# The first weight unit of a decoder layer: finer transfers, the squares of x on ScalarE, matmuls on zeros, products reordered

## The chip, the cores and the metric

The kernel runs on one core of a Trainium2 chip. The metric is the device time of one execution in microseconds, the median of several runs. The profile is of one execution.

## What is computed

One decoder layer on x of 512 tokens by 1024 channels, float32: a half-weighted SwiGLU feed-forward with 2816 hidden channels, a mixing part (gated linear attention and dilated attention side by side), a second feed-forward, and a final norm. What matters here is how it begins:

```python
def rms_norm(x, g):
    xf = x.astype(jnp.float32)
    y = xf * lax.rsqrt(jnp.mean(xf * xf, axis=-1, keepdims=True) + EPS)
    return (y * g.astype(jnp.float32)).astype(x.dtype)

def swiglu(x, w1, w3, w2):
    return (jax.nn.silu(x @ w1) * (x @ w3)) @ w2

x = x + 0.5 * swiglu(rms_norm(x, ffn1_norm[l]), ffn1_w1[l], ffn1_w3[l], ffn1_w2[l])
```

## The kernel before

x is held transposed, as 8 positions of 128 channels by 512 tokens. A float32 product is made of three: both sides are split into a high part, rounded to the matmul's type, and the rest, and hi by hi, hi by lo and lo by hi are added up in a PSUM bank (`product`, L968 to 972). So a tile of output, 128 channels by 512 tokens, takes 8 positions of three matmuls (`tile_of`, L974).

Weights come in units of 1 MB (in the first feed-forward: 128 rows of 2048 columns, the first 1024 for w1, the rest for w3). SyncE loads them alternately into `raw[0]` and `raw[1]` (`load`, L267), each as soon as VectorE has split the unit before it in that buffer (semaphore `w_split`). ScalarE rounds a unit to `w_hi` (`split`, L369 to 371; counted by `w_round`), VectorE subtracts to get `w_lo` (L590, 591; counted by `w_split`), and TensorE runs through the unit's two tiles. Units 0 and 1 use banks 0 to 3, unit 2 uses bank 0 again, so it needs VectorE to have emptied that (`tile_out`).

The norm's factor is applied behind the matmul: h is x times the gain only (`round_h` on ScalarE, L381, `low_h` on VectorE, L600), and VectorE multiplies each finished bank by `rstd` (L631, 633). `rstd` needs the sum of squares of x over channels: squares of positions 0 to 3 on ScalarE (L438), added by VectorE (L681); squares of positions 4 to 7 and their additions on GpSimd (L321 to 327); then two products with a matrix of ones behind unit 0 or 1 (L1012, 1014), mean (L617), root (L393), reciprocal (L621), and the clearing of `sumsq` (L607).

Then every tile pair goes gate (L631), silu on ScalarE (L402), prod (L633, 636), rounding and rest of the hidden value (L405, L639). In this step ScalarE (`split_next` in `up`, L403) and VectorE (L637) also split the unit two ahead. Each engine runs its instructions in the written order, so unit 2's split stands behind the mean, the reciprocal and the first gate.

At the start SyncE issues seven transfers: the first half of unit 0 (L277), x as four pairs of positions (L279), the second half of unit 0 (L281), unit 1 (L271), and then constants, `w_a2` and the positions (L283 to 285). ScalarE issues the gains (L428). ScalarE rounds the first half of unit 0 (L430), then the eight h_hi (L383), the second half (L436), four squares (L438), unit 1. VectorE does w_lo of the first half (L669), the eight h_lo (L603), w_lo of the second half (L674), three additions (L681), unit 1. GpSimd computes, behind the sums, the tables for the rotary embedding (L331 to 345).

## Time and profile before

| | |
|---|---|
| median of 3 runs | 1035.94 us (1035.8 to 1037.5) |
| span of the profiled execution | 1035.7 us |
| TensorE busy | 1011.0 us (98%), 4500 matmuls |
| VectorE busy | 497.5 us (48%) |
| ScalarE busy | 333.9 us (32%) |
| GpSimd busy | 67.4 us (7%) |
| DMA | 92.36 MB, mean 89 GB/s |
| mean granted clock of TensorE | 0.993 |

Busy shares are over the whole span. The busy time of TensorE counts from the first matmul of an overlapping run to the end of its last, so it is not the time at its peak. In the timeline, a row gives the start, the time it took, engine and line, what was written from what, and in brackets how long the engine had been idle and whose end released it.

### The profile page before, as it was taken

The numbers are of one execution on the slowest core, as the hardware profiler recorded it, in microseconds if no ns is written. First come the engines' busy times: TensorE is split into PE (matmuls) and PEld (weight loads), VectorE is DVE, ScalarE is ACT, GpSimd is POOL, SyncE is SP. The second block draws the span as 40 slices with busy tenths as digits, with TensorE's granted clock in tenths as the row PEclk, the third lists the DMA queues.
The fourth block names the chain that finished last, engine by engine and source line by source line (L and its number), as shares of the span: only waits on it lengthen the run. The fifth ranks groups of instructions, "written<-read, shape, count | busy, mean of one in ns | idle before, by whom it ended". The sixth has DMA issues, their size and how long they took to land.

```text
span 1035.7 us, 11866 instructions
## 1 busy us (share of the span) xinstructions
PE 1011.0 (98%) x4500; PEld 807.9 (78%) x4500; DVE 497.5 (48%) x641; ACT 333.9 (32%) x412; POOL 67.4 (7%) x47
## 2 busy tenths in 40 slices
PE   5999999999999999999999999999999999999995
PEld 4788888888888877888776577888888888888884
DVE  7654442244443455734267755854534234444343
ACT  5333321122322345412435533533322113222220
POOL 4850000000000000000122110000000000000000
PEclk9999999999999999999999999999999999999997
DMA  6323222323221323222120012232222232221222
GB/s 250 122 81 114 78 72 102 113 90 122 81 79 64 101 101 122 83 87 90 68 81 1 2 41 82 82 122 81 86 96 87 95 112 92 109 95 57 74 72 81
DMA packets 16272, 92.36 MB, mean 89 GB/s; under 512 B 1888, under 2 KB 1904, under 8 KB 8688
## 3 DMA queue, kind: packets, MB, share of 16 engines
q1 hardware_dynamic: 15520, 90.86, 24.8%
q10 hardware_dynamic: 720, 1.07, 0.3%
q8 instruction: 21, 0.34, 0.1%
q14 instruction: 11, 0.09, 0.0%
HBM read 89.82 MB, written 2.10 MB: 89 GB/s over the span
## 4 chain that ended last, share of the span: by engine, by line
PE 95%; DVE 3%; ACT 1%; DMA 0%; issue 0%; DVEq 0%; ACTq 0%
PE bank L970 29%; PE bank L972 28%; PE bank L971 28%; PE bank L1164 2%; PE bank L1152 2%; PE bank L1176 2%; DVE h_lo L603 1%; PE bank L1105 1%; DVE w_lo L591 1%; DMA raw<-in_up 0%; DVE x L962 0%; PE bank L1101 0%; PE bank L1182 0%; DVE rstd L621 0%; PE bank L1074 0%
## 5 line engine op out<-in xcount | busy, mean ns | idle before, releaser
L970 PE MATMUL bank<-h_hi,w_hi 128*128 128x512 f32 x904 | 356.9, 395 | 12.8 <-DVE h_lo L603 10.2
L971 PE MATMUL bank<-h_lo,w_hi 128*128 128x512 f32 x904 | 353.3, 391 | 0.0
L972 PE MATMUL bank<-h_hi,w_lo 128*128 128x512 f32 x904 | 353.3, 391 | 0.0
L371 ACT ACTIVATE w_hi<-raw 128x2048 fp32r<-128x2048 f32 (+2 forms) x92 | 158.0, 1717 | 336.3 <-PE bank L972 336.3
L591 DVE TENSOR_TENSOR w_lo<-raw,w_hi 128x2048 fp32r<-128x2048 f32 (+2 forms) x92 | 189.0, 2054 | 90.6 <-ACT w_hi L371 90.3
L970 PEld LDWEIGHTS bank<-h_hi,w_hi 128*128 128x128 f32 x904 | 170.6, 189 | 55.0 <-DVE w_lo L669 9.0
L972 PEld LDWEIGHTS bank<-h_hi,w_lo 128*128 128x128 f32 x904 | 170.5, 189 | 36.2
L971 PEld LDWEIGHTS bank<-h_lo,w_hi 128*128 128x128 f32 x904 | 170.7, 189 | 35.2 <-issue 0.7
L972 PE MATMUL bank<-g_hi,w_lo 128*128 128x512 f32 x352 | 140.4, 399 | 0.0
L971 PE MATMUL bank<-g_lo,w_hi 128*128 128x512 f32 x352 | 138.7, 394 | 0.0
L970 PE MATMUL bank<-g_hi,w_hi 128*128 128x512 f32 x352 | 138.0, 392 | 0.0
L633 DVE TENSOR_TENSOR prod<-bank,rstd 128x512 f32<-128x512 f32 x44 | 30.4, 691 | 188.1 <-PE bank L972 188.1
L646 DVE SCALAR_TENSOR_TENSOR x<-bank,x 128x512 f32 (+1 forms) x32 | 22.1, 691 | 124.2 <-PE bank L972 124.2
L971 PEld LDWEIGHTS bank<-g_lo,w_hi 128*128 128x128 f32 x352 | 66.1, 188 | 16.9
L970 PEld LDWEIGHTS bank<-g_hi,w_hi 128*128 128x128 f32 x352 | 66.1, 188 | 15.9
L972 PEld LDWEIGHTS bank<-g_hi,w_lo 128*128 128x128 f32 x352 | 66.1, 188 | 15.3
L402 ACT ACTIVATE gate<-gate 128x512 f32<-128x512 f32 x44 | 27.8, 632 | 155.4 <-DVE gate L631 155.4
L352 POOL TENSOR_TENSOR projT<-projT,rope_c 128x512 f32<-128x512 f32 x8 | 13.7, 1732 | 478.9 <-DVE square L726 478.1
L631 DVE TENSOR_TENSOR gate<-bank,rstd 128x512 f32<-128x512 f32 x44 | 30.3, 688 | 27.6 <-PE bank L972 26.7
L639 DVE TENSOR_TENSOR g_lo<-prod,g_hi 128x512 f32 (+1 forms) x44 | 33.1, 752 | 0.0
L636 DVE TENSOR_TENSOR prod<-prod,gate 128x512 f32<-128x512 f32 x44 | 30.5, 693 | 2.5 <-ACT gate L402 0.6
L389 ACT ACTIVATE square<-x 128x512 f32 (+1 forms) x24 | 15.0, 625 | 48.8 <-DVE x L646 41.7
(176 smaller groups left out, 661.4 us busy)
## 6 DMA issues: line engine op xcount, KB each, us to landing
raw<-in_up SPq DMA_DIRECT2D x43, 1024.0 KB, 4.7
raw<-in_w_proj SPq DMA_DIRECT2D x8, 1024.0 KB, 4.8
raw<-in_down1a SPq DMA_DIRECT2D x8, 768.0 KB, 4.3
raw<-in_down2a SPq DMA_DIRECT2D x8, 768.0 KB, 4.3
raw<-in_down1b SPq DMA_DIRECT2D x8, 640.0 KB, 3.8
raw<-in_down2b SPq DMA_DIRECT2D x8, 640.0 KB, 3.9
raw<-in_w_v SPq DMA_DIRECT2D x4, 1024.0 KB, 4.8
raw<-in_w_o SPq DMA_DIRECT2D x4, 1024.0 KB, 4.8
```

The lines of the kernel that those rows point to most:

```text
L371: nc.scalar.activation(w_hi[u % 2][:, 0:size], raw[u % 2][:, 0:size], ACT.Copy).then_inc(w_round, 1)
L402: nc.scalar.activation(gate[:], gate[:], ACT.Silu).then_inc(silu_done, 1)
L591: nc.vector.tensor_tensor(w_lo[u % 2][:, 0:size], raw[u % 2][:, 0:size], w_hi[u % 2][:, 0:size].bitcast(F32), ALU.subtract).then_inc(w_spl ...
L631: nc.vector.tensor_tensor(gate[:], ps[2 * j][:], rstd[:], ALU.mult).then_inc(tile_out, 1)
L633: nc.vector.tensor_tensor(prod[:], ps[2 * j + 1][:], rstd[:], ALU.mult).then_inc(tile_out, 1)
L636: nc.vector.tensor_tensor(prod[:], prod[:], gate[:], ALU.mult).then_inc(g_mul, 1)
L639: nc.vector.tensor_tensor(g_lo[:, f, :], prod[:], g_hi[:, f, :].bitcast(F32), ALU.subtract).then_inc(g_ready, 1)
L646: nc.vector.scalar_tensor_tensor(x[:, m, :], ps[4 + j][:], 0.5, x[:, m, :], ALU.mult, ALU.add).then_inc(tile_out, 1)
L970: nc.tensor.matmul(out, a_hi, b_hi, start=first, stop=False)
L971: nc.tensor.matmul(out, a_hi, b_lo, start=False, stop=False)
L972: return nc.tensor.matmul(out, a_lo, b_hi, start=False, stop=last)
L1152: nc.tensor.matmul(ps[4 + i % 2][:, 0:(i + 1) * P], projT[r:r + HD, T_AQ + 2 * (h // 2), i * P:(i + 1) * P], projT[r:r + HD, T_AK + 2 * (h ...
```

## The change

- The first half of unit 0 comes in two transfers, of 256 and 768 columns, and x in eight transfers of one position each. The order is w part 0, x0, w part 1, x1, x2 to x7, then as before. Each part and each position has its own semaphore.
- ScalarE rounds part 0, then h_hi 0, part 1, h_hi 1, and the rest of h_hi; VectorE follows in the same order.
- GpSimd squares nothing. ScalarE squares positions 0 and 1 ahead of unit 1 and positions 2 to 7 behind it, into eight buffers; VectorE adds all up, seven additions, behind w_lo of unit 1. One product with ones, behind the first tile of unit 1, sums them.
- Unit 2's split stands on both engines ahead of the norm's mean and the first gate, no more in the first `up` step. The first two `up` steps are written out ahead of the loop.
- VectorE clears `rope_c`, and TensorE multiplies it three times into bank 7, which nothing reads, ahead of the first product.
- In unit 0's first tile, TensorE does hi by hi of position k+1 ahead of the two products with lo of position k. In the next two tiles all products with `w_hi` stand ahead of those with `w_lo`, so that only these wait for `w_split`.

```diff
-        first_squares = [sumsq, square, rstd, ffn_mem[1][2]]
+        first_squares = [sumsq, square, rstd, ffn_mem[1][2], ffn_mem[1][3], rope_s, part, turn]
+        FIRST_COLS = ((0, 2 * P), (2 * P, D))
...
-                    sp.dma_start(raw[0][:, 0:D], source(0)[:, 0:D]).then_inc(w_first, 16)
-                    for j in range(4):
-                        sp.dma_start(x[:, 2 * j:2 * j + 2, :],
-                                     xT_in[2 * j:2 * j + 2].rearrange("c p s -> p c s")).then_inc(x_in[j], 16)
+                    for j, (lo, hi) in enumerate(FIRST_COLS):
+                        sp.dma_start(raw[0][:, lo:hi], source(0)[:, lo:hi]).then_inc(w_first[j], 16)
+                        sp.dma_start(x[:, j, :], xT_in[j]).then_inc(x_in[j], 16)
+                    for m in range(2, KC):
+                        sp.dma_start(x[:, m, :], xT_in[m]).then_inc(x_in[m], 16)
...
-            for m in range(KC // 2, KC):
-                pool.wait_ge(x_in[m // 2], 16)
-                if m == KC // 2:
-                    step(nc.gpsimd.tensor_tensor(rope_s[:], x[:, m, :], x[:, m, :], ALU.mult))
-                else:
-                    step(nc.gpsimd.tensor_tensor(part[:], x[:, m, :], x[:, m, :], ALU.mult))
-                    step(nc.gpsimd.tensor_tensor(rope_s[:], rope_s[:], part[:], ALU.add))
...
             act.wait_ge(w_in[0], 16)
             nc.scalar.activation(w_hi[0][:, D:UP_W], raw[0][:, D:UP_W], ACT.Copy).then_inc(w_round, 1)
-            for m, out in enumerate(first_squares):
-                nc.scalar.activation(out[:], x[:, m, :], ACT.Square).then_inc(first_sq, 1)
+            for m in range(2):
+                square_first(m)
             split(1, 0, unit_size(1))
+            for m in range(2, KC):
+                square_first(m)
+            split_next(0, 0, 2)
             ffn(0, 0, 0, ffn_mem[1][0], ffn_mem[1][2], ffn_mem[1][3], G_MIX)
...
+            nc.vector.memset(rope_c[:], 0.0).then_inc(warm_zero, 1)
...
-            for m in range(1, KC // 2):
+            split(1, 0, unit_size(1))
+            for m in range(1, KC):
                 dve.wait_ge(first_sq, m + 1)
                 if m > 1:
                     dve.wait_ge(first_sum, m - 1)
                 nc.vector.tensor_tensor(sumsq[:], sumsq[:], first_squares[m][:], ALU.add).then_inc(first_sum, 1)
-            split(1, 0, unit_size(1))
+            split_next(0, 0)
             ffn(0, 0, 0, *ffn_mem[1], G_MIX)
...
+                    def first_unit():
+
+                        for pos in range(KC + 1):
+                            if pos < KC:
+                                pe.wait_ge(first_round, min(pos // 2 + 1, 2))
+                                pe.wait_ge(h_round, pos + 1)
+                                nc.tensor.matmul(ps[0][:], w_hi[0][:, pos * P:pos * P + P], h_hi[:, pos, :],
+                                                 start=pos == 0, stop=False)
+                            if pos:
+                                k = pos - 1
+                                pe.wait_ge(first_split, min(k // 2 + 1, 2))
+                                pe.wait_ge(h_ready, k + 1)
+                                nc.tensor.matmul(ps[0][:], w_hi[0][:, k * P:k * P + P], h_lo[:, k, :],
+                                                 start=False, stop=False)
+                                last = nc.tensor.matmul(ps[0][:], w_lo[0][:, k * P:k * P + P], h_hi[:, k, :],
+                                                        start=False, stop=k == KC - 1)
+                        last.then_inc(tile_done, 1)
+                        pe.wait_ge(tile_out, BANK_CREDIT)
+                        late_low(0, 1, 1, lambda: pe.wait_ge(w_round, 1), lambda: pe.wait_ge(w_split, 1))
+
+                    def late_low(slot, w, bank, rounded, split):
+
+                        rounded()
+                        for k in range(KC):
+                            col = (w * KC + k) * P
+                            nc.tensor.matmul(ps[bank][:], w_hi[slot][:, col:col + P], h_hi[:, k, :],
+                                             start=k == 0, stop=False)
+                            nc.tensor.matmul(ps[bank][:], w_hi[slot][:, col:col + P], h_lo[:, k, :],
+                                             start=False, stop=False)
+                        split()
+                        for k in range(KC):
+                            col = (w * KC + k) * P
+                            last = nc.tensor.matmul(ps[bank][:], w_lo[slot][:, col:col + P], h_hi[:, k, :],
+                                                    start=False, stop=k == KC - 1)
+                        last.then_inc(tile_done, 1)
+
+                    def second_unit():
+
+                        late_low(1, 0, 2, lambda: pe.wait_ge(w_round, 2), lambda: pe.wait_ge(w_split, 2))
+                        pe.wait_ge(const_landed, 32)
+                        pe.wait_ge(first_sum, KC - 1)
+                        channel_sums(0, 6, sumsq[:])
+                        tile_of(1, 1, 3)
...
+            pe.wait_ge(warm_zero, 1)
+            for _ in range(WARM):
+                nc.tensor.matmul(ps[7][:], rope_c[:, 0:P], rope_c[:], start=True, stop=True)
             ffn(0, 0, 0, *ffn_mem[1])
```

## Rows read from the trace of the kernel before

**Rows 1.** The page: TensorE's busy time, and its costliest group of instructions.
```profile
PE 1011.0 (98%) x4500; PEld 807.9 (78%) x4500; DVE 497.5 (48%) x641; ACT 333.9 (32%) x412; POOL 67.4 (7%) x47
...
L970 PE MATMUL bank<-h_hi,w_hi 128*128 128x512 f32 x904 | 356.9, 395 | 12.8 <-DVE h_lo L603 10.2
```
**Rows 2.** The timeline, TensorE (PE matmul, PEld weight load), 9 to 41 us.
```profile
9.02 0.77 PE L970 MATMUL bank<-h_hi,w_hi 128*128 128x512 f32 x1 [9.02 <-DVE h_lo L603]
...
14.84 0.19 PEld L970 LDWEIGHTS bank<-h_hi,w_hi 128*128 128x128 f32 x1 [0.43 <-DVE h_lo L603]
...
19.97 0.19 PEld L970 LDWEIGHTS bank<-h_hi,w_hi 128*128 128x128 f32 x1 [1.45 <-DVE w_lo L674]
...
27.17 1.02 PE L1012 MATMUL bank<-sumsq,const 128*128 128x512 f32 x2
...
40.59 0.19 PEld L970 LDWEIGHTS bank<-h_hi,w_hi 128*128 128x128 f32 x1 [1.04 <-issue]
```
**Rows 3.** The waits of 0 to 60 us (in total, times, longest).
```profile
PE bank L970 <- DVE h_lo L603: 10.2, 3, 9.0
```
**Rows 4.** VectorE: line 603's durations (ns min/median/max), then the timeline, 21 to 45 us.
```profile
L603 DVE SCALAR_TENSOR_TENSOR h_lo<-x,gains,h_hi x8: 746/1524/1776, 8.1 to 16.2; 128x512 fp32r<-128x512 f32 x8
...
21.71 0.69 DVE L681 TENSOR_TENSOR sumsq<-sumsq,rstd 128x512 f32<-128x512 f32 x1
22.51 0.69 DVE L681 TENSOR_TENSOR sumsq<-sumsq,gate 128x512 f32<-128x512 f32 x1
23.12 2.29 DVE L591 TENSOR_TENSOR w_lo<-raw,w_hi 128x2048 fp32r<-128x2048 f32 x1
29.08 0.69 DVE L617 TENSOR_SCALAR rstd<-bank 128x512 f32<-128x512 f32 x1 [3.68 <-PE bank L1014]
...
34.40 0.63 DVE L631 TENSOR_TENSOR gate<-bank,rstd 128x512 f32<-128x512 f32 x1
...
37.53 2.92 DVE L591 TENSOR_TENSOR w_lo<-raw,w_hi 128x2048 fp32r<-128x2048 f32 x1 [0.95 <-ACT w_hi L371]
...
44.80 2.29 DVE L591 TENSOR_TENSOR w_lo<-raw,w_hi 128x2048 fp32r<-128x2048 f32 x1 [1.02 <-ACT w_hi L371]
```
**Rows 5.** The timeline, GpSimd, its first work on x.
```profile
10.04 1.05 POOL L324 TENSOR_TENSOR rope_s<-x 128x512 f32<-128x512 f32 x1 [9.61 <-DMA x<-in_xT]
```
**Rows 6.** Windows of 1 us: busy by engine, granted clock (PEclk), DMA share, GB/s.
```profile
21.00:22.00 1.00, 1.00 (x4) 0.79 (x3) 0.89 (x2) 0.00 (x0) 0.05 (x1) 0.50 0.80 172
...
23.00:24.00 1.00, 1.00 (x4) 0.76 (x4) 1.00 (x2) 0.00 (x0) 0.00 (x0) 0.56 0.95 401
```
**Rows 7.** Transfers: issues of L279 (x), L271 (units from 1 on), landing of gains last.
```profile
L279 SPq DMA_DIRECT2D x<-in_xT x4: 423/517/585, 1.2 to 2.8; - x4
...
DMA to landing us min/median/max: 6.1/7.4/8.5
...
L271 SPq DMA_DIRECT2D raw<-in_up x6: 333/338/576, 4.1 to 56.3; - x6
...
DMA to landing us min/median/max: 4.7/4.7/11.0
...
DMA to landing us min/median/max: 5.3/5.3/5.3
```
**Rows 8.** Windows of 1 us, columns as in rows 6, two early microseconds.
```profile
2.00:3.00 1.00, 0.00 (x0) 0.00 (x0) 0.00 (x0) 0.47 (x1) 0.00 (x0) 1.00 0.90 247
...
10.00:11.00 1.00, 1.00 (x4) 0.80 (x3) 1.00 (x2) 1.00 (x2) 0.96 (x1) 1.00 1.07 422
```
**Rows 9.** The timeline, ScalarE, 7 to 18 us.
```profile
7.34 5.32 ACT L383 ACTIVATE h_hi<-x,gains 128x512 fp32r<-128x512 f32 x8 [0.39 <-DMA x<-in_xT]
12.60 1.06 ACT L436 ACTIVATE w_hi<-raw 128x1024 fp32r<-128x1024 f32 x1
13.57 0.61 ACT L438 ACTIVATE sumsq<-x 128x512 f32<-128x512 f32 x1
...
15.65 1.89 ACT L371 ACTIVATE w_hi<-raw 128x2048 fp32r<-128x2048 f32 x1
```

More of the change, by code:

```diff
@@ L153, in layer_program @@
         ps = [ctx.enter_context(nc.psum_tensor(f"bank{b}", [P, S], F32)) for b in range(8)]
-        x_in = [sem(f"x_in{j}") for j in range(4)]
+        x_in = [sem(f"x_in{j}") for j in range(KC)]
         gains_in_sem = sem("gains_landed")
         const_landed = sem("const_landed")
-        w_first = sem("w_first")
+        w_first = [sem(f"w_first{j}") for j in range(2)]
+        warm_zero = sem("warm_zero")
         pos_landed = sem("pos_landed")
@@ L659, in ffn @@
                         clear_sums()
-                    with dve.Fori(0, n // 2 - 1) as i:
+                    peeled = u0 == 0
+                    if peeled:
+                        up(0, 0, True)
+                        up(0, 1)
+                    with dve.Fori(int(peeled), n // 2 - 1) as i:
                         for j in range(2):
@@ L1007, in up @@
                                 channel_sums(NORM[layer], 6, sumsq[:])
-                        if first and layer == 0:
-                            pe.wait_ge(const_landed, 32)
-                            pe.wait_ge(first_sum, KC // 2 - 1)
-                            nc.tensor.matmul(ps[6][:], ones, sumsq[:], start=True, stop=False)
-                            pe.wait_ge(pool_step, KC - 1)
-                            nc.tensor.matmul(ps[6][:], ones, rope_s[:], start=False, stop=True).then_inc(sums_done, 1)
+                    def first_unit():
[16 more added lines that the diff above has]
+                        late_low(0, 1, 1, lambda: pe.wait_ge(w_round, 1), lambda: pe.wait_ge(w_split, 1))
```

53 lines of the change are left out of this document (33 added, 20 removed).

## The prediction

> **What bounds the kernel now.** I read the page first, then the waits, then the first 60 us of the timeline engine by engine. The page says that TensorE is busy for 1011.0 of 1035.7 us [rows 1]: outside a few places it is the bound, and whatever brings it sooner into its unbroken run shifts all that follows by the same amount. One matmul costs 1011.0 / 4500 = 0.225 us of that, though the line's mean is 395 ns [rows 1], because they overlap; a unit of 48 costs 10.8 us. The diff touches only what lies before unit 2 of the weights, so the question is one number: when does TensorE start on unit 2? In the timeline it starts on unit 0 at 9.02, and starts on unit 2 at 40.59, after a gap of 1.04 [rows 2]. Units 0 and 1 hold 96 matmuls, 96 x 0.225 = 21.6 us, and the sums of squares some 2 us (two products of about 1 us, the first at 27.17) [rows 2]: 24 us of work in 31.6 us of time. The rest is waiting, and the low clock.
>
> The waits name the cause: of the 10.2 us that TensorE waited for h_lo, 9.0 lie before the first matmul [rows 3], and then each position waits for VectorE. VectorE needs 1524 ns in the median for one h_lo, 746 at best and 1776 at worst [rows 4]. The long ones lie where GpSimd is at work on its squares, from 10.04 on [rows 5]. The Trainium skill ("SBUF — State Buffer", the section on the two separate sides) says that a VectorE instruction with two SBUF inputs and a GpSimd instruction that reads SBUF hold a shared pair of ports for their whole length, so that one blocks the other. By that, the trace agrees: the median h_lo is a GpSimd operation longer than the shortest, or nearly so.
>
> The clock plays a part too. TensorE's gaps between the last positions grew from 0.43 us at 14.84 to 1.45 at 19.97 (four in all) [rows 2], and behind them the granted clock reads 0.50, that is 1.2 GHz, at 21 to 22 us, and 0.56 in the microsecond from 23 to 24 [rows 6]. At that level a unit costs twice as much.
>
> At 40.59 what released TensorE was w_lo of unit 2, a 2.92 us subtraction that began at 37.53 [rows 4]. It was queued on ScalarE and VectorE behind the norm and the first gate. So today two chains set the start of unit 2: this split, and the chain sums, mean, root, reciprocal, first gate, which frees bank 0 (from 29.08 to 34.40 + 0.63 = 35.03) [rows 4].
>
> **The change part by part.** I follow the bytes, then ScalarE, VectorE and TensorE.
>
> Transfers. Up to the end of unit 1 the same 4.19 MB move, in 12 transfers instead of 7. In the trace the x pairs were issued from 1.2 to 2.8 us and landed 6.1 to 8.5 us after issue, so x was whole at about 11.3; unit 1 was issued at 4.1 and took 11.0 us, so it landed at 15.1 [rows 7]. An issue takes 0.42 to 0.59 us [rows 7]; ten more of these ahead of unit 1 put its issue near 6 us, far ahead of its bytes, so the rate of the queue remains the limit and I leave 15.1 where it is. The first quarter of w (0.13 MB) and x0 (0.26 MB) land earlier than the first 0.52 MB did; but the gains, which took 5.3 us [rows 7] from an issue at 0.73, land at 6.0, and h_hi of position 0 needs them. The rate was 247 GB/s at 2 to 3 us and 422 at 10 to 11 [rows 8]. The Trainium skill ("DMA: Bandwidth & Descriptors", Bandwidth) speaks against finer transfers: batch to at least 1 MiB for three quarters of the peak. The trace's 512 KB transfers, queued back to back, moved at the 422 GB/s, so by the row the sum does not change; by the rule it is the second rival below.
>
> ScalarE. h_hi of position 0 runs from 6.05 to 6.7 (eight took 5.32, 0.66 each) [rows 9], the rest of w_hi's first half needs 0.8, then seven h_hi of 0.66: done at 12.2, just behind the last x. The second half of w_hi stays at 12.60 [rows 9], for its bytes come no sooner. Two squares at 0.52 apart (four between 13.57 and 15.65) [rows 9] end at 14.7. Unit 1 now starts when it lands, 15.1, and takes 1.89 [rows 9]: 17.0. Six squares more: 20.2. These six are the four of GpSimd and two of ScalarE's own that stood ahead before; moved behind unit 1 they delay nobody, since VectorE is busy until 19.3. Unit 2's load waits for w_lo of unit 0 (now near 14.9 instead of 19.9) and takes 4.7 us at best [rows 7], with some 0.8 MB of constants and positions still ahead of it: 2 us at 422 GB/s, so it lands near 21. Its rounding ends at about 22.9.
>
> VectorE. Without GpSimd, h_lo goes at its minimum of 746 ns; eight of them and the two pieces of w_lo end at 13.6 instead of 17.9, and w_lo's second half at 14.9. Then unit 1: 17.1 plus 2.29 [rows 4] gives 19.3. The seven additions, 0.80 apart (21.71 to 22.51) [rows 4], where three stood before, start at 19.3, the last at 24.1: four more on the path, 3.2 us, is the price of taking the squares from GpSimd. Unit 2's split starts 0.61 behind the last one's start (as 23.12 behind 22.51) [rows 4] and takes 2.29: 27.0. Then comes the mean, and from the mean's start to the end of the first gate it takes the 5.95 us of today (29.08 to 35.03) [rows 4], GpSimd's rope table running beside it in both cases: **32.95**.
>
> TensorE. The three products on zeros run from about 1.4 to 6.5 at the worst: a whole fp32 product takes about 1.0 us [rows 2], twice that at 1.2 GHz. They end before h_hi of position 0 at 6.7, so they cost nothing; and they may bring the clock up. From 8.2 on (h_hi of position 1) a position costs 3 x 0.225 = 0.68 of TensorE and 0.75 of VectorE, so TensorE keeps pace. Tile 0 ends at 14.2, tile 1 at 19.6, tile 2 at 25.0, the sum at 26.0 and tile 3 at 31.4. The hi products ahead of the split matter little for the end: they cover that w_lo of unit 0's second half comes at 14.9 and unit 1's at 19.3. If the clock were low until 12 us, TensorE would end unit 1 at about 32.6, still inside its cover of 1.6 us; without that cover each lost us counts.
>
> The sum: unit 2 needs its split (27.0), TensorE (31.4) and bank 0 (32.95). The last decides: TensorE starts at 33.0 instead of 40.59, **7.6 us sooner**. Next to be late would be unit 3's split. Today w_lo of unit 3 starts 10.4 us behind the first gate's start (34.40 to 44.80) [rows 4]; with the split of unit 2 gone from between (2.9 and its wait of 0.95 less, g_hi's wait of 0.7 more) that is some 7.8, and its end 10 to 11 us behind the gate's start at 32.3: 42.4 to 43.4. TensorE wants it at 33.0 + 10.8 = 43.8. It fits, with GpSimd's collisions as the danger; I give it 0 to 0.8 us. The profiled span of 1035.7 is 0.24 below the median of the runs, 1035.94. Against the span the result is 1028.1, against the median **1028.4**.
>
> **The rivals.**
> The clock falls in the new gap. TensorE idles from 31.4 to 33.0. For: at 21 us the clock was 0.50 after four gaps of 0.4 to 1.5 us [rows 2, 6]. Against: the 1.04 us gap before 40.59 [rows 2] brought no fall, and here there is one gap, not four. The low level began in the microsecond behind 19.97, and with 0.56 from 23 to 24 [rows 6] it ended near 23.9: some 3.5 us, which at half speed cost 1.7. Result 1030.1 to 1030.6.
>
> The transfers are slower. If unit 2's load took the 11.0 us of unit 1 [rows 7] rather than 6, it would land at 26, be rounded at 28 and split at 30.3; with the 5.95 us behind it, 36.3: a gain of 4.3. The same comes out if fine transfers keep the 247 GB/s of the start [rows 8] up to 3.15 MB: 14.7 instead of 11, so all is 3.7 us later. Against: the rate rose while transfers of the same 2 KB rows were in flight. Result 1032.
>
> Better than forecast: unit 1 lands sooner, or VectorE's additions are closer together than 0.80. TensorE's own end of unit 1, 31.4, is the floor: 1026.8.
>
> Nothing comes of it: the start of unit 2 stays where it was, because VectorE, with four more additions and the split ahead of the mean, hands bank 0 over late. This needs 7 us on a chain that I put together from 14 durations of this trace: unlikely.
>
> Slower: the clock stays at 1.2 GHz through both units. The first matmul, at 9.02, has 0.77 us [rows 2], twice the mean of its line [rows 1]: TensorE starts slow. If the positions, paced by VectorE, never pack closely enough to end that, 95 matmuls from 8.2 at 0.45 and a doubled sum give 8.2 + 42.8 + 2 = 53.0, 12.4 later than today: 1048.3. It becomes slower than today once TensorE has lost more than 9.2 us against 31.4, that is with 41 matmuls more at the low level than the forecast has. Against: tiles 1 to 3 have all their inputs and run without gaps, and after the fall near 20 us such a run brought the clock back before 24 [rows 6].
>
> **How the numbers follow.** Forecast 0.58 (1027.4 to 1029.4), clock dip 0.17, slower transfers 0.10, better 0.07, nothing 0.04, slower 0.04. The range takes in the better case and the dip and ends inside the slower transfers: 1026.4 to 1031.6. A measurement of this kernel can tell about 0.2% (2 us) from no change. Faster by more than that: 0.58 + 0.17 + 0.10 + 0.07 = 0.92; within it 0.04; slower 0.04.
>
> **What would show it.** In the profile after: h_lo at about 0.75 us each and no GpSimd before 26 us; w_lo of unit 1 at 17.1; seven additions from 19.3 to 24.8; w_lo of unit 2 at 24.7, ahead of the mean at 27.0; the first gate's end at 33; TensorE's first matmul of unit 2 right behind it, and a wait of about 1.5 us there that names VectorE's gate. From there every row stands 7.6 us earlier. It is wrong if unit 1 lands later than 15.5, if the clock reads 0.50 anywhere from 14 to 40 us, or if w_lo of unit 3 ends after 44.

## The result, and the profile after

The kernel before took 1036.72 us in the comparison (median of 4 runs, 1035.8 to 1037.63), the changed one 1030.06 us (4 runs, 1029.84 to 1030.88). The ratio is 0.994, with a 95% interval of 0.9926 to 0.9955. The forecast was 1028.4 with a range of 1026.4 to 1031.6: the direction and the range held, the size was 1.7 us too hopeful against this time. Against the 1035.94 us that stood at the outset the gain is 5.9 us, where 7.6 were forecast.

The profiled execution has a span of 1028.7 us. Its page, to be read beside [rows 1], gives busy time by engine, the line of the granted clock in 40 slices, and the costliest group:

```profile
PE 1012.5 (98%) x4504; PEld 807.9 (79%) x4504; DVE 494.0 (48%) x647; ACT 331.5 (32%) x413; POOL 57.4 (6%) x40
...
PEclk9999999999999999999999999999999999999997
...
L992 PE MATMUL bank<-h_hi,w_hi 128*128 128x512 f32 x880 | 345.4, 392 | 2.4 <-DVE gate L644 1.4
```

TensorE is busy for 1.5 us more, the products on zeros included. Its costliest line waits 2.4 us in all where it waited 12.8. The two are not quite alike, for the first three tiles' products now have lines of their own (880 of the 904 are left); but on those lines the matmuls wait only 0.4 us, for an h_hi, and nowhere in the first 60 us does TensorE wait for h_lo any more. The clock's digit is 9 (90% or more) in every slice but the last, to which I come back; the line reads the same in the kernel before, for a dip of 3 us does not show in slices of 26.

The timeline of TensorE in the changed kernel, to 33 us (the row gives the start, the time it took, the line, and in brackets the idle time before it and its releaser); the rows that it answers to are [rows 2]:

```profile
1.48 5.49 PE L1090 MATMUL bank<-rope_c 128*128 128x512 f32 x6 [1.48 <-DVE rope_c L686]
5.98 1.34 PE L1032 MATMUL bank<-h_hi,w_hi 128*128 128x512 f32 x1
...
30.80 0.39 PE L994 MATMUL bank<-h_hi,w_lo 128*128 128x512 f32 x1
...
32.58 0.19 PEld L992 LDWEIGHTS bank<-h_hi,w_hi 128*128 128x128 f32 x1 [1.81 <-DVE gate L644]
```

Unit 2 starts at 32.58 instead of 40.59 [rows 2], right behind the first gate and behind the longest gap of the beginning, 1.81 us. The waits name the same releaser (engine and line, waited for whom: in total, times, longest):

```profile
PEld bank L992 <- DVE gate L644: 1.8, 1, 1.8
...
PE bank L992 <- DVE gate L644: 1.4, 1, 1.4
```

VectorE in the changed kernel, the rows that answer to [rows 4]:

```profile
7.86 4.73 DVE L616 SCALAR_TENSOR_TENSOR h_lo<-x,gains,h_hi 128x512 fp32r<-128x512 f32 x7
...
16.78 2.29 DVE L604 TENSOR_TENSOR w_lo<-raw,w_hi 128x2048 fp32r<-128x2048 f32 x1 [2.12 <-ACT w_hi L369]
18.99 0.69 DVE L703 TENSOR_TENSOR sumsq<-sumsq,square 128x512 f32<-128x512 f32 x1
...
23.77 0.69 DVE L703 TENSOR_TENSOR sumsq<-sumsq,turn 128x512 f32<-128x512 f32 x1
24.38 2.29 DVE L604 TENSOR_TENSOR w_lo<-raw,w_hi 128x2048 fp32r<-128x2048 f32 x1
26.58 0.68 DVE L630 TENSOR_SCALAR rstd<-bank 128x512 f32<-128x512 f32 x1
...
31.89 0.63 DVE L644 TENSOR_TENSOR gate<-bank,rstd 128x512 f32<-128x512 f32 x1
...
39.40 2.29 DVE L604 TENSOR_TENSOR w_lo<-raw,w_hi 128x2048 fp32r<-128x2048 f32 x1 [1.11 <-ACT w_hi L369]
...
43.79 0.69 DVE L646 TENSOR_TENSOR prod<-bank,rstd 128x512 f32<-128x512 f32 x1
```

Seven h_lo take 4.73 us with GpSimd idle; from the last addition to the end of the gate (31.89 + 0.63) every row stands 0.3 to 0.4 us ahead of the forecast and in its order. Against the kernel before the lead is 8.03 us at 43.79 (the same instruction stood at 51.82) and lasts until the final norm. There the two kernels part once more. Windows of 1 us, the changed kernel (busy share and count of PE, PEld, DVE, ACT, POOL, then the granted clock, DMA share, GB/s):

```profile
1013.00:1014.00 1.00, 0.61 (x6) 0.65 (x6) 0.00 (x0) 0.24 (x1) 0.00 (x0) 1.00 0.00 0
1014.00:1015.00 1.00, 1.00 (x7) 1.00 (x6) 0.00 (x0) 0.00 (x0) 0.00 (x0) 0.52 0.00 0
1015.00:1016.00 1.00, 1.00 (x7) 1.00 (x6) 0.00 (x0) 0.00 (x0) 0.00 (x0) 0.50 0.00 0
```

In the kernel before the clock fell 0.6 us behind the same sums, not inside them:

```profile
1022.00:1023.00 1.00, 1.00 (x11) 1.00 (x11) 0.00 (x0) 0.00 (x0) 0.00 (x0) 1.00 0.00 0
1023.00:1024.00 1.00, 0.36 (x4) 0.28 (x3) 0.33 (x2) 0.20 (x1) 0.00 (x0) 0.99 0.00 0
1024.00:1025.00 1.00, 0.00 (x0) 0.00 (x0) 0.86 (x6) 0.00 (x0) 0.00 (x0) 0.50 0.00 0
```

The sums of the final norm come 7 a microsecond instead of 11, and the lead shrinks from 8.03 to 7.01 us (the last products of the norm start at 1018.55, before at 1025.56). The other three executions of the changed kernel have spans of 1027.7, 1027.9 and 1027.9, some 0.9 shorter than the profiled one, and a mean granted clock of 0.994 against its 0.993; that these did not lose the microsecond at the end is inferred from the two.

### The profile page after: what moved, and what is told of

Same layout as the page of the kernel before. It is cut to its first block, busy times and chain, and to the rows that moved or that the text cites. A ratio compares the mean times of both kernels' runs of the same rounds, so it can differ in the third digit from the quotient of the medians.

```text
span 1028.7 us, 11872 instructions
## 1 busy us (share of the span) xinstructions
PE 1012.5 (98%) x4504; PEld 807.9 (79%) x4504; DVE 494.0 (48%) x647; ACT 331.5 (32%) x413; POOL 57.4 (6%) x40
## 4 chain that ended last, share of the span: by engine, by line
PE 95%; DVE 3%; DMA 1%; SPq 0%; ACT 0%; issue 0%; DVEq 0%; ACTq 0%
PE bank L992 29%; PE bank L994 28%; PE bank L993 28%; PE bank L1224 2%; PE bank L1212 2%; PE bank L1236 2%; DMA raw<-in_up 1%; PE bank L1165 1%; DVE w_lo L604 1%; DVE sumsq L703 0%; DVE x L984 0%; PE bank L1161 0%; PE bank L1242 0%; DVE rstd L634 0%; PE bank L1134 0%
## 5 line engine op out<-in xcount | busy, mean ns | idle before, releaser
L992 PE MATMUL bank<-h_hi,w_hi 128*128 128x512 f32 x880 | 345.4, 392 | 2.4 <-DVE gate L644 1.4
L993 PE MATMUL bank<-h_lo,w_hi 128*128 128x512 f32 x880 | 342.5, 389 | 0.0
L994 PE MATMUL bank<-h_hi,w_lo 128*128 128x512 f32 x880 | 342.5, 389 | 0.0
L992 PEld LDWEIGHTS bank<-h_hi,w_hi 128*128 128x128 f32 x880 | 165.2, 188 | 41.8 <-issue 3.1
L994 PEld LDWEIGHTS bank<-h_hi,w_lo 128*128 128x128 f32 x880 | 165.2, 188 | 34.4
L993 PEld LDWEIGHTS bank<-h_lo,w_hi 128*128 128x128 f32 x880 | 165.2, 188 | 34.4 <-issue 0.7
L993 PEld LDWEIGHTS bank<-g_lo,w_hi 128*128 128x128 f32 x352 | 66.1, 188 | 17.1
L387 ACT ACTIVATE square<-x 128x512 f32 (+1 forms) x24 | 15.0, 625 | 48.8 <-DVE x L660 41.7
```

The source lines that it names most:

```text
L992: nc.tensor.matmul(out, a_hi, b_hi, start=first, stop=False)
L993: nc.tensor.matmul(out, a_hi, b_lo, start=False, stop=False)
L994: return nc.tensor.matmul(out, a_lo, b_hi, start=False, stop=last)
```

## The experiments

Eleven variants were run, and the kernel before once more for a second trace of it. Every ratio is against the kernel before, run among the same runs. None leaves out a part of the layer's computation; the products at the end, like the zeros, write a bank that nobody reads, and GpSimd's early write is of a tile that is overwritten before use.

| | us, median | start of unit 2, us |
|---|---|---|
| before | 1035.8 to 1037.3 | 40.59 (39.04 in a second trace) |
| changed | 1030.06 | 32.58 |
| no products on zeros | 1031.42 | 32.75 |
| unit 2's split as before | 1037.3 | 37.10 |
| GpSimd squares again | 1035.06 | 38.12 |
| before, with the early split alone | 1035.86 | 39.67 |
| transfers as before | 1031.9 | 34.42 |
| products in the old order | 1030.47 | 32.87 |
| sums earlier | 1029.69 | 32.09 |
| products at the end | 1029.37 | as changed |
| sums earlier, constants later | 1028.47 | no gap left |
| all three | 1027.58 | no gap left |
| one early GpSimd write | 1030.33 | as changed |

### Without the products on zeros

```diff
-WARM = 3
+WARM = 0
```

> The changed kernel without the three products on zeros. In the changed kernel TensorE idles 1.81 us before unit 2 (from 30.77 to 32.58), waiting for the first gate; the zeros ran from 1.48 to 6.9 and the clock was full from the second real product on. Theory (the zeros buy a full clock early, and the idle time covers most of it): without them TensorE runs its first 4 us or more at 1.2 GHz, ends unit 1 some 2 us later, the sum of squares too, so the mean starts up to 1 us later than 26.58 and unit 2 begins at 33.0 to 33.6: 0.4 to 1.0 us slower than the changed kernel. Rival (zeros do nothing): unit 2 still begins at 32.6. Second rival (the clock never settles while positions are paced by VectorE): unit 2 begins after 36.

Measured: 1031.42 us (1030.62 to 1031.67), ratio 0.9955 (0.9938 to 0.9972). The timeline of TensorE:

```profile
8.05 0.77 PE L1032 MATMUL bank<-h_hi,w_hi 128*128 128x512 f32 x1 [1.81 <-ACT h_hi L381]
8.61 0.63 PE L1038 MATMUL bank<-h_lo,w_hi 128*128 128x512 f32 x1
9.04 0.63 PE L1040 MATMUL bank<-h_hi,w_lo 128*128 128x512 f32 x1
...
11.16 0.39 PE L1038 MATMUL bank<-h_lo,w_hi 128*128 128x512 f32 x1
11.39 0.39 PE L1040 MATMUL bank<-h_hi,w_lo 128*128 128x512 f32 x1
```

Until 11 us the products come 0.43 us apart, behind that 0.23. Half speed for 3 us costs TensorE 1.5 us, and in this execution nearly all of it lies inside idle time: unit 2 starts at 32.75, 0.17 later. But the cover is not the 1.6 us ahead of unit 2 alone. The mean needs the sum of squares, and this ended at 25.71 in the changed kernel, 0.9 us before the mean; here it ends at 26.71 and the mean starts at 26.75, so that any further loss of TensorE would delay mean, gate and unit 2 by the same amount. The profiled execution is the fastest of the four; the others are 0.5 to 1.0 longer in span. The likely reason, not shown, is that in these the half speed lasted longer: in the two traces of the kernel before it lasted until 13.4 us in one and 12.2 in the other. A different loss at the end of the kernel is the rival, and nothing here rules it out. The median is 1.4 us above that of the changed kernel, from four runs of each whose ranges overlap a little (1030.62 to 1031.67, 1029.84 to 1030.88), though the traced beginning says 0.2.

### Unit 2's split behind the first gate again

```diff
-                        up(0, 0, True)
+                        up(0, 0)
...
-            split_next(0, 0)
             ffn(0, 0, 0, *ffn_mem[1], G_MIX)
```

(The same edit on ScalarE.)

> The changed kernel with unit 2's split back at its old place, behind the norm and inside the first up step. Theory (this order is the largest single part): the mean starts when the sum of squares is out, 25.8 instead of 26.58, the first gate ends near 31.7, but the split follows it: ScalarE from 31.9 to 33.8, VectorE's subtraction from 33.8 to 36.1 or 36.7. Unit 2 begins at 36.2 to 37.2: 3.6 to 4.6 us slower than the changed kernel. Rival (the gate is what matters, the split is hidden beside it): unit 2 begins near 32, no slower.

Measured: 1037.3 us (10 runs, 1036.97 to 1038.18), ratio 1.0013 (1.0004 to 1.0023): slower than the kernel before. The wait, the split itself, and 1 us windows from 35 us:

```profile
PE bank L990 <- DVE w_lo L603: 6.0, 1, 6.0
```
```profile
34.14 2.83 DVE L603 TENSOR_TENSOR w_lo<-raw,w_hi 128x2048 fp32r<-128x2048 f32 x1 [1.01 <-ACT w_hi L369]
```
```profile
35.00:36.00 1.00, 0.00 (x0) 0.00 (x0) 1.00 (x1) 0.00 (x0) 1.00 (x1) 0.77 0.00 0
36.00:37.00 1.00, 0.00 (x0) 0.00 (x0) 1.00 (x2) 0.00 (x0) 1.00 (x1) 0.50 0.00 0
...
41.00:42.00 1.00, 1.00 (x4) 0.71 (x4) 0.80 (x1) 0.69 (x2) 0.92 (x2) 0.50 0.16 66
```

The split ends near 37.0 and unit 2 starts at 37.10, inside the expected range and 4.5 us later than with the whole change. The median is 7.2 us longer, though. During the wait (6.0 us without a product, 6.4 between weight loads) the clock falls, it reads 0.50 from 36 to 42 us, and TensorE's first 5.3 us of unit 2 run at half speed, which costs 2.65. 4.5 + 2.65 = 7.2. (The two traced spans are only 6.1 apart, for the traced changed kernel lost its 1.0 us at the end, and this one did not.) So the early split is the largest of the parts that were taken out one by one, and it is worth more than the wait that it removes.

### GpSimd squares positions 4 to 7 again

```diff
+            for m in range(KC // 2, KC):
+                pool.wait_ge(x_in[m], 16)
+                ...
-            for m in range(1, KC):
+            for m in range(1, KC // 2):
                 dve.wait_ge(first_sq, m + 1)
```

> The changed kernel with the squares of positions 4 to 7 back on GpSimd and two products with ones, three additions on VectorE instead of seven. Theory (GpSimd's work slows VectorE's h_lo): GpSimd works from about 8.7 to 18, h_lo goes from 0.69 to about 1.5 us each, the last ends near 16 instead of 12.6, the first tile near 16.7 instead of 13.2; TensorE passes the end of the sums some 4.5 us later (3.5 from the tile, 0.9 for the second product), so the mean starts near 30 and unit 2 begins at 35 to 36: 2.5 to 3.5 us slower. Rival (the four additions saved on VectorE, 3.2 us, pay for the slower h_lo): unit 2 begins within 0.5 us of 32.6.

(ScalarE's four squares and four of the additions go with it, and the second product with ones comes back.)

Measured: 1035.06 us (10 runs, 1033.53 to 1036.4), ratio 0.9984 (0.9975 to 0.9994). VectorE in this kernel, beside the 4.73 and 2.29 us of the changed one:

```profile
7.71 9.31 DVE L623 SCALAR_TENSOR_TENSOR h_lo<-x,gains,h_hi 128x512 fp32r<-128x512 f32 x7
...
18.93 3.37 DVE L611 TENSOR_TENSOR w_lo<-raw,w_hi 128x2048 fp32r<-128x2048 f32 x1
```

From one h_lo to the next it is 1.33 us against 0.68. That is the contention on which the prediction rested; the other things that this edit moves stand behind the h_lo, so it is GpSimd's work that lengthens them. The size was a miss: unit 2 starts 5.5 us later (38.12), not 2.5 to 3.5. The subtractions are lengthened too (3.37 for 2.29), and TensorE waits for each h_lo in turn, five times from 10 to 17 us. Behind these gaps the granted clock falls. The waits of 0 to 25 us, then the windows:

```profile
PE bank L1045 <- DVE h_lo L623: 3.2, 5, 1.0
```
```profile
17.00:18.00 1.00, 0.83 (x3) 0.71 (x4) 1.00 (x2) 0.99 (x2) 0.92 (x1) 0.73 0.05 18
18.00:19.00 1.00, 1.00 (x4) 0.81 (x3) 1.00 (x2) 0.00 (x0) 1.00 (x1) 0.50 0.00 0
...
20.00:21.00 1.00, 1.00 (x4) 0.77 (x3) 1.00 (x1) 0.00 (x0) 0.14 (x1) 0.57 0.76 131
```

The low time in the four windows from 17 to 21 adds up to 3.4 us, and half speed over that time costs 1.7.

### The kernel before with the early split alone

```diff
+                    peeled = u0 == 0
+                    if peeled:
+                        up(0, 0, True)
+                        up(0, 1)
...
+            split_next(0, 0)
             ffn(0, 0, 0, *ffn_mem[1], G_MIX)
```

> The kernel before with one part of the change alone: unit 2's split ahead of the mean and the first gate on both engines. Theory (the parts don't add up: alone, this one meets TensorE's own late end of unit 1 at 39.6): unit 2 begins at 39.6 to 39.8 instead of 40.59, 0.8 to 1.0 us faster than before, though the same order is worth 4 us in the changed kernel. Rival (the parts add up): 3.6 us or more faster than before. Second rival (the split ahead delays mean and gate by 2.3 us, and this decides): the gate ends at 37.3, before 39.6, so nothing is lost by it; if unit 2 begins later than 40.6 this is wrong.

Measured: 1035.86 us (10 runs, 1034.88 to 1036.6), ratio 0.9994 (0.9984 to 1.0003). The kernel before has two sorts of executions, with spans near 1034.1 and near 1035.7 (below). Here four of the ten spans are near 1033.1, three are 1034.8 and three lie between; the two ends are 0.9 to 1.0 us below those of the kernel before, as expected. In VectorE's rows the split now holds the mean up, since its load comes late, and the first gate follows:

```profile
29.39 2.62 DVE L597 TENSOR_TENSOR w_lo<-raw,w_hi 128x2048 fp32r<-128x2048 f32 x1 [3.88 <-ACT w_hi L371]
31.94 0.68 DVE L623 TENSOR_SCALAR rstd<-bank 128x512 f32<-128x512 f32 x1
...
37.24 0.63 DVE L637 TENSOR_TENSOR gate<-bank,rstd 128x512 f32<-128x512 f32 x1
```

TensorE's weight load for unit 2:

```profile
39.67 0.19 PEld L982 LDWEIGHTS bank<-h_hi,w_hi 128*128 128x128 f32 x1
```

The mean came at 29.08 before [rows 4]. But the split is done at 32.0 and the gate at 37.9, and neither decides: TensorE goes from unit 1 into unit 2 at 39.67 with no idle time in the row. What bounds this kernel is TensorE's own late way through units 0 and 1, which is why the early split alone brings 1 us. Taken out of the whole change it costs 7. The parts don't add up: the split pays in full only once TensorE itself is through unit 1 early.

### Transfers as before

```diff
-                    for j, (lo, hi) in enumerate(FIRST_COLS):
-                        ...
+                    sp.dma_start(raw[0][:, 0:D], source(0)[:, 0:D]).then_inc(w_first[0], 16)
+                    for j in range(4):
+                        sp.dma_start(x[:, 2 * j:2 * j + 2, :],
+                                     xT_in[2 * j:2 * j + 2].rearrange("c p s -> p c s")).then_inc(x_in[j], 16)
```

> The changed kernel with the transfers of before: the first half of unit 0 in one, x in four pairs. Theory (finer transfers start the chain sooner, but the chain that decides hangs on unit 1's landing): h_hi of position 0 starts near 7.3 instead of 4.54, the last h_lo ends near 14.2 instead of 12.6, unit 1 lands at 15.1 as before; TensorE passes the sum some 1.4 us later, so the mean starts 0.2 to 0.7 us later than 26.58 and unit 2 begins at 32.8 to 33.3: 0.2 to 0.7 us slower. Rival (fine transfers cost rate): unit 1 lands sooner with coarse ones and unit 2 begins before 32.6.

Measured: 1031.9 us (5 runs, 1031.32 to 1032.32), ratio 0.996 (0.9946 to 0.9974); unit 2 starts at 34.42, 1.84 later, where 0.2 to 0.7 were expected. The timeline of TensorE, then the windows:

```profile
1.48 5.25 PE L1089 MATMUL bank<-rope_c 128*128 128x512 f32 x6 [1.48 <-DVE rope_c L685]
8.25 0.47 PE L1031 MATMUL bank<-h_hi,w_hi 128*128 128x512 f32 x1 [1.53 <-ACT h_hi L380]
9.60 0.61 PE L1031 MATMUL bank<-h_hi,w_hi 128*128 128x512 f32 x1 [0.87 <-ACT h_hi L380]
```
```profile
9.00:10.00 1.00, 0.40 (x1) 0.39 (x2) 1.00 (x2) 1.00 (x3) 0.00 (x0) 0.88 1.07 412
10.00:11.00 1.00, 1.00 (x4) 0.79 (x3) 1.00 (x2) 1.00 (x3) 0.00 (x0) 0.50 1.08 428
```

The mean, on VectorE:

```profile
28.43 0.69 DVE L629 TENSOR_SCALAR rstd<-bank 128x512 f32<-128x512 f32 x1 [1.32 <-PE bank L1008]
```

The first product comes 2.3 us later than the 5.98 of the changed kernel, since the first bytes of x do: h_hi of position 0 starts at 7.39, there at 4.54. TensorE idles between the zeros and it, and once more behind it, and the clock, at 0.88 in the first window, reads 0.50 from 10 to 13 us. The bulk of the bytes is hardly late: unit 1's rounding starts at 15.27 here and at 14.83 in the changed kernel. Those 0.44 us carry through to the end of unit 2's split (27.11), and they are what the expected 0.2 to 0.7 was made of. The mean waits 1.32 us longer, for TensorE's sum of squares, and that wait is the rest of the 1.8. TensorE is late for two reasons, the last h_lo (14.48 instead of 12.59) and the clock (3.4 us low, of which some 1.5 us of delay are left, since h_lo would have held TensorE up a little even at full speed). Without the clock's part the sum, out at 28.39, would have been out at about 26.9, an estimate from these rows, ahead of the split. So most of what the finer transfers are worth here, some 1.3 of 1.8 us, comes from the clock, because TensorE is kept at work early. They lost nothing of the rate: 416 and 442 GB/s at 9 to 11 us with single positions, 412 and 428 with pairs.

### Products in the old order

First tile position by position, then `tile_of` for the others, as in the kernel before.

```diff
-                        late_low(1, 0, 2, lambda: pe.wait_ge(w_round, 2), lambda: pe.wait_ge(w_split, 2))
+                        pe.wait_ge(w_split, 2)
+                        tile_of(1, 0, 2)
```

> The changed kernel with the products in the old order: no hi product ahead, and tiles 1 and 2 wait for w_lo before they start. Theory: tile 1 waits for w_lo of unit 0's second half until 14.7 instead of starting at 13.3, so everything on TensorE is 1.2 to 1.5 us later up to the sum; the sum is out near 27.0 instead of 25.7, the mean 0.4 us later, unit 2 begins near 33.0: 0.4 us slower. Rival (the order is worth its full 1.4 us): unit 2 begins at 34. Second rival (nothing): 32.6.

Measured: 1030.47 us (4 runs, 1030.31 to 1031.04), ratio 0.9947 (0.993 to 0.9964). Unit 2 starts at 32.87, 0.3 later: tile 1 waits 1.46 us for its split and starts at 14.81, and this shows through only where the sums follow it. The new order is worth 0.3 to 0.4 us, which these runs (four of each) hardly tell from nothing.

### Sums earlier

From here on the experiments go beyond the change: what is late now is the chain sums, mean, gate. Three squares and two of the seven additions stand ahead of unit 1's split, the clearing of `sumsq` behind the gate, and the product with ones in the middle of tile 2.

```diff
+            for m in range(1, KC):
+                if m == 3:
+                    split(1, 0, unit_size(1))
...
+                            if k == KC // 2 and between:
+                                between()
```

> The changed kernel with its deciding chain shortened: squares 0 to 2 ahead of unit 1 on ScalarE, two of the seven additions in VectorE's idle time ahead of unit 1's split, the sum of squares taken in the middle of tile 2's products with w_lo, and the clearing of the sum behind the first gate instead of ahead of it. Theory (the chain additions, split of unit 2, mean, root, reciprocal, gate decides): the five additions end near 22.9 instead of 24.5, the mean starts near 25.1, the gate ends 2.0 us sooner, and TensorE, whose own end of unit 1 is 30.8, begins unit 2 at 30.8 to 31.2 instead of 32.58: 1.4 to 1.8 us faster than the changed kernel. Rival (the next to be late is unit 3's split, which ended at 41.7 where TensorE wanted it at 43.5): half of the gain is lost again at 41.7. Second rival: no gain, since TensorE was the bound.

Measured: 1029.69 us (4 runs, 1029.32 to 1030.07), ratio 0.9937 (0.992 to 0.9954). Unit 2 starts at 32.09, not at 30.8 to 31.2. The rows of ScalarE and VectorE name the new bound:

```profile
22.42 1.92 ACT L369 ACTIVATE w_hi<-raw 128x2048 fp32r<-128x2048 f32 x1 [2.83 <-DMA raw<-in_up]
```
```profile
24.37 2.29 DVE L604 TENSOR_TENSOR w_lo<-raw,w_hi 128x2048 fp32r<-128x2048 f32 x1 [1.26 <-ACT w_hi L369]
```

ScalarE had been idle for 2.83 us when unit 2's bytes landed at 22.4. In the changed kernel they landed at 20.7; why 1.7 us sooner there I did not settle. In both they stand in the queue behind 1.2 MB of constants and positions (the prediction had counted 0.8), and the next experiment takes those out of their way.

### Constants and positions behind unit 2

This stands on top of the sums earlier.

```diff
-                    sp.dma_start(const[:], const_in).then_inc(const_landed, 16)
+                    sp.dma_start(const[:, 0:C_STRIP], const_in[:, 0:C_STRIP]).then_inc(const_landed, 16)
...
+                    load(0, 1, source(2))
+                    sp.dma_start(const[:, C_STRIP:N_CONST], const_in[:, C_STRIP:N_CONST]).then_inc(const_rest, 16)
```

> The kernel with the sums taken earlier, and in addition all constants but the identity and the ones, and the positions, are loaded behind unit 2 of the weights instead of ahead of it. There, unit 2 landed at 22.4 us (VectorE idled 1.26 us for it) and TensorE began unit 2 at 32.09 instead of the 31.0 expected. Theory (unit 2's load is what came late, behind 1.05 MB nobody needs yet): it lands 2 us or more sooner, at 19.7 to 20.5, its split starts at 22.9 to 23.0, the mean when the sum is out, near 25.0, the gate ends near 30.5, and TensorE begins unit 2 at 30.9 to 31.2, with no wait or one of 0.2 us: 1.5 us faster than the changed kernel (0.9 faster than with the sums alone). Rival (unit 3's split, which ended at 41.3 there, now comes late, since its load moves behind the constants): TensorE waits at 41.8 to 42.5 and gives half of it back.

Measured: 1028.47 us (4 runs, 1028.42 to 1028.52), ratio 0.9923 (0.9908 to 0.9938), 1.6 below the changed kernel. Unit 2's rounding starts at 19.61 instead of 22.42, the mean at 25.09, the first gate at 29.86, and TensorE goes from tile 3 into unit 2 with no gap. TensorE's own work is the bound from 8 us on, the floor that the rival "better" of the prediction named; its time of 1026.8 is too low by the step that failed, as below. Unit 3's split, whose load now stands behind the constants, was in time: TensorE has no idle time there.

### Products that keep the clock up at the end

Seven products ahead of the last sums and nine behind them, into a bank that nobody reads:

```diff
+            idle_products(7)
             pe.wait_ge(sq_added, 9 * 2 + KC)
...
+            idle_products(9)
             spread(1, 6, ffn_mem[2][4])
```

> The changed kernel with products nobody reads in TensorE's two idle times at the very end, 7 ahead of the final sums and 9 ahead of the spread of the norm. In the changed kernel the granted clock fell at 1014.0, in the kernel before at 1024.0, and in the profiled pair 1.0 of 8.0 us of the lead was lost right there, since the eight sums ran at 0.43 instead of 0.22 apart. Theory (the clock falls in the tail and costs there): the sums stay at 0.22 and the spread takes 1.1 instead of 2.1 us; the whole is 1.0 to 2.0 us faster than the changed kernel. Rival (the extra products delay the sums): if the clock falls all the same, nine products at 0.43 take 3.9 us where 2.3 are idle, and the kernel is 1.6 us slower.

Measured: 1029.37 us (4 runs, 1029.02 to 1030.43), ratio 0.9939 (0.9922 to 0.9955), 0.7 below the changed kernel, where 1.0 to 2.0 were expected. The expectation was made from the profiled execution, which had lost a microsecond more at the end than the others. The last product of the norm, here and then in the changed kernel:

```profile
1017.64 1.16 PE L1277 MATMUL bank<-norm_diag,const 128*128 128x128 f32 x8
```
```profile
1018.55 2.08 PE L1277 MATMUL bank<-norm_diag,const 128*128 128x128 f32 x8 [2.21 <-DVE norm_diag L869]
```

Eight matmuls in 1.16 us against 2.08: the end of the kernel was running at the low clock (0.50 from 1015 us on), and with the unread products it reads 1.00 until 1023.

### All three

Sums earlier, constants later and the products at the end together.

> Sums earlier, constants later, and the products in the tail's idle time, together. Theory: the start gives 1.5 us against the changed kernel and the tail 0.7 (as measured alone), and the two don't touch: 2.2 us faster than the changed kernel, near 1027.9 us, 8 us faster than before. Rival: the time in the tail depends on where the clock falls, so the sum may be 1.2 to 3.0.

Measured: 1027.58 us (5 runs, 1027.41 to 1028.7), ratio 0.9914 (0.99 to 0.9927): 2.5 below the changed kernel, where 2.2 were expected. It beats both kernels. The products at the end are no guarantee: in the profiled run, the slowest of the five, the clock fell in spite of them (0.74, 0.50, 0.50 and 0.55 in the four windows from 1014 us).

### The kernel before, a second trace

> The kernel before, unchanged, profiled once more. Of 25 runs of it 18 took 1035.7 to 1036.1 us with spans near 1034.1, and 7 took 1037.3 to 1037.6 with spans near 1035.7. The profile on which the prediction rests has a span of 1035.7. Theory (that profile is of the longer sort, and the difference is the low clock from 20.5 to 23.9 us): a profile with a span of 1034.1 shows no clock of 0.50 between 14 and 30 us, and TensorE ends the sums of squares and unit 1 some 1.6 us sooner, with unit 2 starting near 38.9. Rival (the difference lies elsewhere, in the tail or the middle): unit 2 starts at 40.6 in the short sort too.

Measured: 1036.3 us (10 runs, 1035.75 to 1037.63), ratio 1.0001. Six of the ten have spans of 1034.0 to 1034.7, four of 1035.6 to 1035.8; among its runs beside the other experiments, 7 of 25, 1 of 8, 6 of 15 and 4 of 7 were of the longer sort. The profiled one here is of the shorter. Its windows, a weight load and the mean, to be held against [rows 6], [rows 2] and [rows 4]:

```profile
21.00:22.00 1.00, 1.00 (x7) 0.79 (x6) 0.89 (x2) 0.00 (x0) 0.13 (x1) 1.00 0.70 164
...
23.00:24.00 1.00, 1.00 (x6) 0.84 (x5) 1.00 (x2) 0.00 (x0) 0.00 (x0) 1.00 0.95 401
```
```profile
14.91 0.19 PEld L970 LDWEIGHTS bank<-h_hi,w_hi 128*128 128x128 f32 x1 [1.13 <-DVE h_lo L603]
```
```profile
27.53 0.69 DVE L617 TENSOR_SCALAR rstd<-bank 128x512 f32<-128x512 f32 x1 [2.05 <-PE bank L1014]
```

No 0.50 here: seven matmuls from 21 to 22 us where the first trace had four. The mean comes 1.55 us earlier, and unit 2 starts at 39.04 instead of 40.59, so the dip accounts for 1.55 of the 1.6 us between the two traced spans. That it also parts the executions that were not traced is inferred from their spans. The gaps are alike except the first, 1.13 us here and 0.43 at 14.84 there [rows 2]: the half speed of the start ended sooner in this execution (12.2 against 13.4 us), so TensorE waited longer for h_lo. The execution with the longer idle time is the one that kept its clock.

### One early write by GpSimd

The time outside the span (device time less span) is 1.74 to 1.84 us in every run of the kernel before, but 2.1 to 2.2 in the changed one. The kernels with GpSimd's squares have the small value (1.77 to 1.86 with the squares put back, 1.74 to 1.83 with the early split alone). Does an idle GpSimd cause the rest?

```diff
+            pool.wait_ge(x_in[4], 16)
+            step(nc.gpsimd.memset(ang[:], 0.0))
```

> The changed kernel with one write by GpSimd of a tile near 9 us (nobody's input), so that GpSimd does work early, as it did before the change, without holding VectorE up. Theory: the 0.35 us by which the time outside the span grew (1.8 to 2.1-2.2 us) belongs to a GpSimd that has done nothing before 25 us; time minus span is 1.8 here, and the time is about 0.35 us below the changed kernel's 1030.06. Rival: it stays 2.1 to 2.2, the time stays, and the cause of the 0.35 us remains open. Unit 2's first full-speed product stays at 32.6 in both.

Measured: 1030.33 us (4 runs, 1030.09 to 1030.9), ratio 0.994 (0.9923 to 0.9956). The spans are 1027.6 to 1028.5, as in the changed kernel, and the time outside them is 2.4 to 2.49 us: it rose. The theory fell, and its rival, no change, did not come out either. With constants later it is 2.51 to 2.54, and with all three together it varies from 2.20 to 2.58 over five runs of one kernel. What sets it is open; the 0.35 us is there in every run of the changed kernel, and it is not part of the beginning.

## Why the prediction came out as it did

**What bounds the kernel, and h_lo.** Right. h_lo takes 0.75 us in every instance (0.68 from one start to the next), GpSimd's first work on data stands at 25.77, and putting the squares back brings 1.33 us each. The prediction costed only h_lo's contention; the run with the squares back shows w_lo of unit 1 lengthened by 1.1 us too. Its reading of the size was loose: the median h_lo stood 0.78 us above the shortest, and the GpSimd instructions beside it took 1.05 to 1.62.

**Transfers.** 15.1 was said for unit 1; ScalarE took it up at 14.83. The gains were said to land at 6.0 and hold h_hi of position 0 to 6.05; they took 3.2 us instead of 5.3, and it started at 4.54. That bound was wrong, and harmless. The rival of slow fine transfers fell: 416 and 442 GB/s at 9 to 11 us. What the prediction did not price at all is what the finer transfers are worth for the clock, some 1.3 us.

**ScalarE and VectorE.** Within 0.5 us throughout: w_lo of unit 1 at 16.78 (said 17.1), additions from 18.99 (19.3), the last at 23.77 (24.1), w_lo of unit 2 at 24.38 (24.7), the mean at 26.58 (27.0), and from there to the gate's end 5.94 us (5.95). The offset of 0.3 is that of unit 1's landing, carried through.

**TensorE.** Tile 3 ended at 31.19 (30.80 + 0.39; said 31.4), the matmuls' wait for the gate is 1.4 us (said 1.5), unit 2 starts at 32.58 (said 33.0). Unit 3's split was in time: it starts at 39.40 and ends at 41.7 where TensorE needs it at 43.4. It started 7.5 us behind the gate's start; the prediction said 7.8, but its own terms (10.4 - 2.9 - 0.95 + 0.7) add up to 7.25. The zeros "cost nothing" was right, though not for its reason: h_hi of position 0 was ready at 5.3, not 6.7, and the first product waited for the zeros until 5.98 (5.48 without them); TensorE then had to wait for position 1 anyway. "The cover of 1.6 us" for a slow start was wrong. It was counted at the start of unit 2; the mean waits for TensorE's sum of squares, and there the cover is 0.9 us. With transfers as before it was used up, and the mean waited 1.32 us.

**The step that failed** is the last one, how the profiled span stands to the median of the runs: "the profiled span of 1035.7 is 0.24 below the median". A span was held against a device time. The two differ by 1.8 us in every run of the kernel before, so a span of 1035.7 belongs to a time of 1037.5, the longer sort: the top of the 1035.8 to 1037.5 that stood at the outset, not the median. The profile that the sum was made from holds the dip of the clock at 21 to 24 us [rows 6], and the prediction itself priced it at 1.7 us, as a rival, without asking whether the median execution has it. The trace of the shorter sort, to which most runs belong, has not: 39.04 to 32.58 is 6.5 us, against 8.0 in the traced pair. The 1036.72 of the comparison lies between two runs of either sort, so it stands for neither.

With that step mended the sum goes: span 1035.7 - 7.6 = 1028.1, and 1.8 outside it, 1029.9; less 0.4 for the better start; plus 0.35 by which the time outside the span grew (open); 1029.9 in all, against 1030.06 measured. The 0.2 left is as much as single spans vary (1027.7 to 1027.9). The end of the kernel can take a further microsecond, in the profiled execution it did. That the measured time lies inside the stated range is in part the width that the rivals gave it; the forecast itself was 1.7 us low, and the 0.4 us by which the start came sooner than said hid some of the error.

**The rivals.** "The clock falls in the new gap" fell as a mechanism: from 0 to 46 us it reads 1.00 in every microsecond, though its time, 1030.1 to 1030.6, is nearest to the measured one. A time that fits is no evidence for the cause. "Slower: the clock stays low" fell, but a fall of the clock behind gaps came with three of the parts taken out: between weight loads 6.4 us (the split late), 2.8 and 1.2 (transfers as before), or five of 0.7 to 1.4 (GpSimd's squares) stood ahead of 3 to 7 us at the low clock. "Better" was reached only with the sums earlier and the constants later.

## What to carry to other kernels

Before a forecast is set against a median, ask which execution the trace is of: take time less span for one run, add it to the trace's span, and see where that falls among the times. If the trace holds a dip of the clock, price the change with it and without it. Count the cover of a slow stretch at every place where another engine waits for TensorE, not only at the last. A part of a change that removes a wait of TensorE may be worth the wait and the slow stretch behind it; and parts that hand work to one another (the split, its load, the engine that feeds it) have to be tried from the whole downwards as well as one by one.

## What the runs showed of the hardware

- A gap's length alone did not decide whether TensorE's clock fell. Behind four gaps between weight loads, of 0.43 to 1.45 us in 6 us, it fell to 1.2 GHz in one trace of the kernel before, and behind four of 0.92 to 1.45 it did not in the other; by the sorts of their spans it fell in 1 of 8 to 4 of 7 executions. One gap of 1.81 us did not bring the fall in the trace of the changed kernel; one of 6.4 us did, and there the low level outlasted the gap by 5.3 us of full work.
- At the start the products come at half speed until 11 us (0.43 us apart) while the granted clock reads 1.00, in the kernel without zeros:

```profile
9.00:10.00 1.00, 1.00 (x4) 0.76 (x3) 1.00 (x3) 1.00 (x3) 0.00 (x0) 1.00 1.07 418
```

  Four matmuls in a microsecond where six fit at full speed: the durations are those of the low level (0.43 us apart, as at 0.50 later in these traces), and the column says the high one. The Trainium skill ("TensorE: Matmul & The Clock Gate", Seeing it yourself) warns that the clock events of a trace were seen to be unreliable on trn2. By these durations, the trace agrees.
- With GpSimd at work on SBUF, h_lo takes twice as long (1.33 us from start to start for 0.68) and a two-input subtraction half as long again (3.37 us for 2.29).
- The time outside the span is the same to 0.12 us over the runs of each kernel but one, and from 1.8 to 2.5 us by the kernel; with all three experiments together it varied by 0.38. No row explains it.
